# Hybrid decoder step: centred values in mLSTM and retention, the head norm taken on undivided numerators, and the four mLSTM denominators on four column tiles

## The reference, cut to what matters

```python
# mLSTM, per head; s = (q k^T) * W
num = einsum(s, v) + a_inter * einsum(q, C)
den = sum(s) + a_inter * einsum(q, n)
h   = num / maximum(abs(den), exp(-m_t))
C_new = a_old * C + einsum(w_end, k, v);  n_new = a_old * n + einsum(w_end, k)
# retention, per head
o = einsum(s, v) + cross
# both: norm over the 128 values of a head
xc = x - mean(x);  y = xc * rsqrt(mean(xc * xc) + eps) * gain
```

## Time and profile before

| what | value |
|---|---|
| median of three runs | 1513.43 us |
| lowest and highest run | 1510.20, 1519.79 us |
| span of the profiled execution | 1509.3 us |
| PE busy | 1479.3 us, 98% of the span |
| DVE, ACT, POOL busy | 770.5, 342.1, 56.2 us |
| DMA | 299.84 MB, mean 199 GB/s |

### The profile page before, as it was taken

How to read it: one execution, slowest core, us unless ns; L and a number is a source line. 1 busy time by engine, 2 the same in 40 slices (tenths; PEclk the granted TensorE clock), 3 DMA queues, 4 the chain that set the end, 5 groups by cost and what they waited for, 6 DMA issues and landing times.

```text
span 1509.3 us, 40728 instructions
## 1 busy us (share of the span) xinstructions
PE 1479.3 (98%) x17933; PEld 1265.3 (84%) x17933; DVE 770.5 (51%) x1700; ACT 342.1 (23%) x855; POOL 56.2 (4%) x68
## 2 busy tenths in 40 slices
PE   9999999999999999999999999999999899999997
PEld 6899976887899999998899977887888787888654
DVE  6446756746665655657366667636662211221123
ACT  2314224222212212233224224123130000000001
POOL 1000010110000000000000010200010000000000
PEclk9999999999999999999999999999999999999999
DMA  8324435203544354256524353114879998999993
GB/s 349 115 88 164 155 139 133 85 25 93 210 154 153 131 188 144 81 207 225 201 100 176 144 150 111 45 44 125 330 314 359 407 360 304 361 355 366 363 385 106
DMA packets 64335, 299.84 MB, mean 199 GB/s; under 512 B 21840, under 2 KB 23568, under 8 KB 37664
## 3 DMA queue, kind: packets, MB, share of 16 engines
q1 hardware_dynamic: 50392, 268.10, 48.5%
q0 software_dynamic: 2944, 18.09, 3.1%
q10 hardware_dynamic: 10823, 11.05, 2.7%
HBM read 277.93 MB, written 19.28 MB: 197 GB/s over the span
## 4 chain that ended last, share of the span: by engine, by line
PE 93%; DVE 3%; DMA 2%; issue 1%; ACT 1%; SPq 0%; DVEq 0%; ACTq 0%
PE ps L2112 15%; PE ps L1250 12%; PE ps L1913 12%; PE ps L1713 9%; PE ps L2035 7%; PE ps L1720 5%; PE ps L1199 4%; PE ps L1825 4%; PE ps L2009 3%; PE ps L1212 2%; PE ps L1787 2%; PE ps L1569 2%; DMA ring<-in_mix 2%; PE ps L1946 2%; PE ps L1265 1%
## 5 line engine op out<-in xcount | busy, mean ns | idle before, releaser
L1713 PE MATMUL ps<-xn,ring 128*128 128x288 f32 x576 | 155.7, 414 | 0.4 <-ACT gate L2478 0.4
L1713 PEld LDWEIGHTS ps<-xn,ring 128*128 128x128 f32 x576 | 105.9, 190 | 37.2 <-issue 10.3
L2112 PE MATMUL ps<-arena 128*128 128x144 f32 x1028 | 133.4, 286 | 1.2 <-DVE arena L3649 1.2
L2112 PEld LDWEIGHTS ps<-arena 128*128 128x128 f32 x1028 | 129.3, 190 | 1.4 <-issue 1.4
L1913 PE MATMUL ps<-y_ml,arena 128*64 128x96 f32 (+4 forms) x2688 | 111.7, 244 | 11.5 <-issue 11.4
L1913 PEld LDWEIGHTS ps<-y_ml,arena 128*64 128x64 f32 x2688 | 109.2, 137 | 15.2 <-issue 15.1
L2035 PE MATMUL ps<-arena,mixed 128*32 128x256 f32 x2024 | 111.3, 380 | 0.0
L2035 PEld LDWEIGHTS ps<-arena,mixed 128*32 128x32 f32 x2024 | 65.0, 110 | 42.3 <-issue 0.2
L3573 DVE TENSOR_TENSOR mixed<-ps,mixed 128x96 f32<-128x96 f32 (+4 forms) x66 | 16.8, 254 | 130.3 <-PE ps L1913 130.1
L1913 PEld LDWEIGHTS ps<-y_ml,ring 128*64 128x64 f32 x1536 | 62.1, 137 | 4.8 <-issue 4.8
L1913 PE MATMUL ps<-y_ml,ring 128*64 128x96 f32 (+4 forms) x1536 | 64.3, 245 | 0.6 <-issue 0.6
(11 more groups left out here) (588 smaller groups left out, 2554.4 us busy)
## 6 DMA issues: line engine op xcount, KB each, us to landing
arena<-in_egu SPq DMA_DIRECT2D x56, 1024.0 KB, 7.4
ring<-in_mix SPq DMA_DIRECT2D x46, 1024.0 KB, 5.5
arena<-in_edown SPq DMA_DIRECT2D x40, 1024.0 KB, 7.3
ring<-in_mix SPq DMA_DIRECT2D x48, 768.0 KB, 4.2
ring<-in_egu SPq DMA_DIRECT2D x32, 1024.0 KB, 7.5
ring<-in_gu SPq DMA_DIRECT2D x14, 1024.0 KB, 4.8
arena<-in_gu SPq DMA_DIRECT2D x8, 1024.0 KB, 5.1
arena<-in_C POOLq DMA_DIRECT2D x2, 2048.0 KB, 7.9
```

The costliest lines, as they stand in the source:

```text
L1713: last = mm(ps[:, bank, 0:T], ring[:, s, P * k:P * k + P], xn[:, k, :], start=(k == 0), stop=(k == KT - 1))
L2112: last = mm(ps[:, dense_bank(side, product), 0:HALF], left, right, start=(k == 0 and product in (1, 2, 5)), stop=(k == n - 1), skip_group_ ...
```

## The change

1. **Values are centred first.** The mean over a head's 128 values is taken off the values instead of off the outputs. DVE sums each token's values (`reduce_sum`, 128x1024 elements); POOL scales the eight sums by -1/128 and adds them to the values into a copy, `mvc` (in the space of `y_ret`) and `rvc` (in the space of `C0`). PE's numerators read the copies. The function `centre` on POOL runs twice a layer, and PE waits for it before the first numerator of each branch. For retention it also waits until the stores of the mLSTM states have landed.
2. **Samples.** Their outputs are centred by two DVE operations: in `sample_outputs` for mLSTM, and in place of ACT's copy for retention.
3. **No centring product.** `centred` is called for RWKV alone. ACT copies and squares each numerator straight out of PSUM.
4. **Denominators once.** PE broadcasts exp(-m) once for the four heads (to 32 rows a head) and makes the four heads' denominators in four column tiles of 32, after the last head. ACT takes one absolute value; DVE makes eps times the square of the denominator.
5. **The norm of the undivided numerator.** The root is taken of mean(num^2) + eps * den^2, so no head is divided by its denominator: three DVE operations a head go.
6. **State n rides with C.** A column of ones stands behind each head's values, so C and n come from one product of 129 columns.
7. **Order.** `COUPLES` becomes rq, rk, mo, mo, zrw 0, zrw 1, rg, rg, then zrw 2 to 6. The norm's steps move: the sums stand at `AT_MLNORM`, six parts lie before the spread; retention's sums stand before the stream's last two parts.

```diff
@@ PE, mlstm_head @@
-                mm(ps[:, 4, 0:TP], picked_head(h), rows[0:NH, 1, 0:TP], start=True, stop=True)
-                mm(ps[:, 5, 0:TP], picked_head(h), rows[0:NH, 2, 0:TP], start=True, stop=True).then_inc(ml_bc.sem, 1)
+                mm(ps[:, 4, 0:TP], picked_head(h), rows[0:NH, 1, 0:TP], start=True, stop=True).then_inc(ml_bc.sem, 1)
...
+                if h == 0:
+                    pe.wait_ge(*v_cent(l, 1))
...
-                for bank, part in ((7, "num"), (4, "den")):
-                    def left(i):
-                        return mvt[:, i, P * h:P * h + P] if part == "num" else C("ones", P)
-                    mm(ps[:, bank, 0:TP], left(0), ml_PW[:, 0:TP], start=True, stop=False, skip_group_check=True)
-                    last = mm(ps[:, bank, P:TP], left(1), ml_PW[:, TP:PW], start=False, stop=True, skip_group_check=True)
-                last.then_inc(ml_nd.sem, 1)
+                mm(ps[:, 7, 0:TP], mvc[:, 0, h, :], ml_PW[:, h, 0:TP], start=True, stop=False, skip_group_check=True)
+                mm(ps[:, 7, P:TP], mvc[:, 1, h, :], ml_PW[:, h, TP:PW], start=False, stop=True,
+                   skip_group_check=True).then_inc(ml_nd.sem, 1)
+
+            def mlstm_denominators(l):
+
+                mm(ps[:, 5, 0:TP], C("sel_s", P, NH), rows[0:NH, 2, 0:TP], start=True, stop=True)
+                for out, weights in ((slice(TP, 2 * TP), slice(0, TP)), (slice(TP + P, 2 * TP), slice(TP, PW))):
+                    for h in range(NH):
+                        last = mm(ps[sample(h), 5, out], C("ones", TS), ml_PW[:, h, weights], start=(out.start == TP),
+                                  stop=(out.start > TP), skip_group_check=True)
+                last.then_inc(ml_dn.sem, 1)
@@ PE, mlstm_state @@
-                for h in range(NH):
-                    for i in range(2):
-                        mm(ps[:, 5, h:h + 1], mkt[:, i, P * h:P * h + P], C("ones", 1), start=(i == 0), stop=(i == 1))
+                        mm(ps[:, 4 + h // 2 * 2, (P + 1) * (h % 2):(P + 1) * (h % 2) + P + 1], mkt[:, i, P * h:P * h + P],
+                           mvt[:, i, h, :], start=(i == 0), stop=(i == 1))
@@ PE, a layer @@
-                centred(3 * l, ml_o, C("cent128", P))
-                steps(l, AT_MLNORM, AT_MLNORM + 4)
+                pe.wait_ge(*ml_oe(l))
                 head_sums(3 * l, ml_sq, C("ones", TS))
-                steps(l, AT_MLNORM + 4, AT_MLNORM + 8)
-                head_spread(3 * l, ml_sq, C("lead", P))
-                steps(l, AT_MLNORM + 8, AT_ROTATE)
+                steps(l, AT_MLNORM, AT_MLNORM + 6)
+                head_spread(3 * l, ml_den, C("lead", P))
+                steps(l, AT_MLNORM + 6, AT_ROTATE)
...
-                centred(3 * l + 1, ret_o, C("cent128", P))
+                pe.wait_ge(*r_ote(l))
+                head_sums(3 * l + 1, ret_sq, C("ones", TS))
                 steps(l, AT_RNORM, NSTREAM)
                 fill(l, 6)
-                head_sums(3 * l + 1, ret_sq, C("ones", TS))
-                fill(l, 8)
-                head_spread(3 * l + 1, ret_sq, C("lead", P))
-                fill(l, 50)
+                head_spread(3 * l + 1, ret_sq[:, 0, :], C("lead", P))
+                fill(l, 58)
@@ ACT @@
-                A(ml_den, ps[:, 4, 0:TP], ACT.Abs).then_inc(ml_ad.sem, 1)
+                A(ml_o[:, h, 0:TP], ps[:, 7, 0:TP], ACT.Copy)
+                A(ml_sq[:, h, 0:TP], ps[:, 7, 0:TP], ACT.Square).then_inc(ml_h.sem, 1)
                 if h == 3:
+                    act.wait_ge(*ml_dn(l))
+                    A(ml_den[:, 0:TP], ps[:, 5, TP:2 * TP], ACT.Abs).then_inc(ml_ad.sem, 1)
...
+            def mlstm_norm(l):
+
+                projections(l, AT_MLNORM, AT_MLNORM + 2)
+                act.wait_ge(*ml_var(l))
+                A(ml_den, ml_den, ACT.Sqrt).then_inc(hn_q.sem, 1)
@@ DVE @@
-                dve.wait_ge(*ml_ad(l, h + 1))
-                link(TT(ml_den, ml_den, ps[:, 5, 0:TP], MAX))
-                link(dve.reciprocal(ml_den, ml_den))
-                TT(ml_o[:, h, 0:TP], ps[:, 7, 0:TP], ml_den, MUL).then_inc(ml_h.sem, 1)
+                if h == NH - 1:
+                    den = ml_den[:, 0:TP]
+                    dve.wait_ge(*ml_ad(l))
+                    link(STT(den, ps[:, 5, 0:TP], MOST, den, MIN, MAX))
+                    link(STT(den, den, GN_EPS, den, MUL, MUL))
...
+            def mlstm_norm(l):
+
+                dve.wait_ge(*hn_sum(3 * l))
+                STT(ml_den, ps[:, 4, 0:T], 1.0 / P, ml_den, MUL, ADD).then_inc(ml_var.sem, 1)
+                couple_add(l, 7, C12)
+                couple_sums(l, 9, 1, 2)
+                dve.wait_ge(hn_q.sem, 3 * l + 1)
+                dve.reciprocal(ml_den, ml_den).then_inc(hn_r.sem, 1)
+                couple_sums(l, 9, 2, 5)
@@ DVE, mlstm_gates after couple_sums(l, 2); mlstm_head h == 1 after kbm; retention after couple_add(l, 12, C11) @@
+                dve.reduce_sum(vsum.rearrange("p (i h) -> p i h", i=2), mvt[:, :, :, 0:P], axis=AX_X).then_inc(v_sum.sem, 1)
...
+                link(dve.reduce_sum(rosum, ps[:, 4, 0:P], axis=AX_X))
+                STT(ros, rosum.broadcast_to([P, P]), -1.0 / P, ps[:, 4, 0:P], MUL, ADD).then_inc(r_ose.sem, 1)
@@ POOL @@
+            def centre(l, n, values, centred, sums):
+
+                sums = sums.rearrange("p (i h) -> p i h", i=2)
+                pool.wait_ge(*v_sum(l, n))
+                pool.tensor_scalar(sums, sums, -1.0 / P, None, ALU.mult).then_inc(v_mean.sem, 1)
+                pool.wait_ge(*v_mean(l, n))
+                pool.tensor_tensor(centred, values, sums.unsqueeze(3).broadcast_to([P, 2, NH, P]), ALU.add)                    .then_inc(v_cent.sem, 1)
...
                 pool.dma_start(S0_ret, a["ret"][l]).then_inc(ld_ret.sem, 16)
+                pool.wait_ge(st_ml.sem, 64 * (l + 1))
+                by_head = [t.rearrange("p i (h e) -> p i h e", h=NH) for t in (rvt, rvc)]
+                centre(l, 4, *by_head, rvsum)
```

More of the change, by code:

```diff
@@ L78 @@
 NORM_EPS, GN_EPS, RW_GN_EPS = 1e-6, 1e-5, 64e-5
+MOST = 1.0e18
 RW_DECAY = 0.606531
@@ L380 @@
 GATE_BANK = (0, 2, 3, 1)
-COUPLES = [("rq", 0), ("rk", 0), ("mo", 0), ("mo", 1), ("rg", 0), ("rg", 1)] + [("zrw", i) for i in range(ZT // 2)]
-NCP = len(COUPLES)
 def projection_stream():
@@ L1277, in head_sums, with head_spread @@
                 last.then_inc(hn_tensor.sem, 1)
[L1279 removed]
+            def head_spread(q, roots, lead):
                 pe.wait_ge(hn_r.sem, q + 1)
                 for j in range(4):
[L1283 removed]
+                    last = mm(ps[:, 4 + j, 0:T], lead[rows_of(j)], roots[rows_of(j), :], start=True, stop=True)
                 last.then_inc(hn_tensor.sem, 1)
@@ L1393, in mlstm_state @@
                 pe.wait_ge(*ml_kb(l))
-                last = mm(ps[:, 5, 8:8 + SB * NH], kts, C("bsel", SB * NH), start=True, stop=True)
+                last = mm(ps[:, 4, 264:264 + SB * NH], kts, C("bsel", SB * NH), start=True, stop=True)
                 last.then_inc(ml_cp.sem, 1)
@@ L2275, in projection @@
                 else:
-                    if part < 2:
-                        dst = (mvt if kind == "mv" else rvt)[:, part, 256 * piece:256 * piece + 256]
-                    else:
-                        dst = (mvs if kind == "mv" else rvs)[:, 0:P]
-                    last = A(dst, ps[:, GROUP_BANK[n], 0:256 if part < 2 else P], ACT.Copy)
+                    if part == 2:
+                        last = A((mvs if kind == "mv" else rvs)[:, 0:P], ps[:, GROUP_BANK[n], 0:P], ACT.Copy)
+                    elif kind == "rv":
+                        last = A(rvt[:, part, 256 * piece:256 * piece + 256], ps[:, GROUP_BANK[n], 0:256], ACT.Copy)
+                    else:
+                        last = A(mvt[:, part, 2 * piece:2 * piece + 2, 0:P],
+                                 ps[:, GROUP_BANK[n], 0:256].rearrange("p (h e) -> p h e", h=2), ACT.Copy)
                 last.then_inc(evac.sem, 1)
@@ L2297, in projections, with retention_norm, rwkv_norm @@
                           scale=DK ** -0.5 if COUPLES[c][0] == "rk" else 1.0).then_inc(c_copy.sem, 1)
[L2299 to L2310 removed]
+            def mlstm_norm(l):
+                projections(l, AT_MLNORM, AT_MLNORM + 2)
+                act.wait_ge(*ml_var(l))
+                A(ml_den, ml_den, ACT.Sqrt).then_inc(hn_q.sem, 1)
+            def retention_norm(l):
+                act.wait_ge(*hn_sum(3 * l + 1))
+                A(ret_sq[:, 0, :], ps[:, 4, 0:T], ACT.Sqrt, scale=1.0 / P, bias=C("eps", 1, P, 1)).then_inc(hn_q.sem, 1)
+                projections(l, AT_RNORM, NSTREAM)
+                unit_gates(l, "norm")
+                unit_gates(l, "shift")
+            def rwkv_norm(l):
+                for j in range(4):
+                    act.wait_ge(*hn_x(l, j + 1))
+                    A(rw_sq[:, j, :], rw_o[:, j, :], ACT.Square).then_inc(hn_s.sem, 1)
+                act.wait_ge(*hn_sum(3 * l + 2))
+                A(rw_sq[:, 0, :], ps[:, 4, 0:T], ACT.Sqrt, scale=1.0 / CH, bias=C("eps", 1, P, 2)).then_inc(hn_q.sem, 1)
```

(25 more changed lines are left out.)

142 lines of the change are left out of this document (68 added, 74 removed).

## The result

The changed kernel takes 1502.99 us (median of 6 runs, 1500.31 to 1506.12), the kernel before 1513.61 (6 runs, 1509.41 to 1519.79). The ratio is 0.9925 with an interval of 0.9901 to 0.9949, so it is faster by 0.75%; the medians lie 10.6 us apart. The forecast was 1497.4, a gain of 16.0. The direction came true. The range, 1491.0 to 1503.0, holds the result by its last 0.01 us, which is luck: single runs of the changed kernel scatter by 5.8. The result lies outside the 1495 to 1499.5 that had the chance of 0.60, and a gain above 1%, which had 0.56, did not come either. A third of the forecast gain is missing, and most of what follows asks where it went.

What follows compares the result with a forecast made beforehand. PE's own list was taken to bound the kernel: 8.21 us a layer less, 16.4 in two, minus 0.4 for waits, gives 16.0 off 1513.43, so 1497.4 us. The range was 1491.0 to 1503.0.

Steps and rivals of the forecast that it cites:

- What bounds the kernel: Whole kernel: PE's own list sets the time, busy 1479.3 of 1509.3 us; loads follow PE.
- PE's own sum: Both layers: PE loses 9.90 us and gains 1.67 and 0.02, net 8.21 us a layer, 16.4 in two.
- rival (a): Denominator tiles do not overlap, or waits in heads 1, 2 or the norm open wider; about 1501 us, chance 0.22.
- Covers of DVE and ACT: Heads and norms: DVE's and ACT's supplies come about when PE needs them; the mLSTM norm's reciprocal is covered by 0.5 us.
- The three tight distances: DVE's supply to PE: head 1 late by 0.1 us, head 2 by 0 to 0.1, mLSTM norm covered by 0.5.
- New waits: Need against supply in the mLSTM and retention branches; all waits put at 0.2 us a layer (0 to 1.5).
- The signs it named: Trace signs: right if PE busy and span fall 16 us; wrong if named PE waits or 2.6 us tiles show.
- falls altogether: mLSTM heads to retention norm: fails if that stretch shrinks under 5 us a layer, or a later one grows.
- The clock: Half-clock dip at 757.00 to 760.00 in layer 1: costs at most 1.5 us, may go or come.
- (b): Experts' stage after 1118 us: loads paced by memory give the gain back; 1510 to 1514 us, chance 0.07.
- (c): POOL's second centring, for retention, is late and PE waits; slower from 19 us of delay a layer, chance 0.02.
- (d): More gain than forecast: added work overlaps, a dip goes, waits elsewhere shrink; 1491 to 1495 us, chance 0.09.

Runs made afterwards that it cites:

- d1: Changed kernel plus sixteen unread centring products on PE ahead of the mLSTM norm's sums, in layer 1 alone; 1514.31 us against 1507.27 for the changed kernel.
- a0: The changed kernel run again without any edit, as the base for experiments on its chip; 1507.27 us, ratio 0.9915 to the kernel before.
- b0: The kernel before the change, run once more for a second profile, which shows no dip of the clock; 1518.99 us.
- e1: Changed kernel with POOL centring retention's values ahead of its wait for y_ml and two loads, eleven us earlier; 1505.13 us, ratio 0.9900 to the kernel before.
- e2: Changed kernel with POOL's addition of the means split into eight 128x128 operations with one tensor input, same place; 1506.99 us, ratio 0.9914 to the kernel before.
- v2b: Changed kernel with the early centring and the two stream parts between heads 0 and 1 set apart, second run; 1505.98 us, ratio 0.9883 to the kernel before.
- p3: Changed kernel with POOL's addition for retention done three times in a row, PE waiting for the last; 1509.95 us, ratio 0.9935 to the kernel before.

## Why the prediction was right, and where it fell short

**What bounds the kernel: right.** d1 shows that time put into PE's list in layer 1 arrives at the end, and what the change takes out of it arrives too: the mixers of a0 are 12.2 us shorter than those of b0, and the medians lie 12.6 apart. For layer 0 no experiment added time; its share is in those two numbers.

**PE's own sum: right.** It said 8.21 us a layer. Up to the rotation the terms are L1364, the denominators, the one-column products and mLSTM's centring product less the additions, 1.72 + 2.60 + 1.68 + 1.95 - 1.69 = 6.26; measured 90.8 - 84.5 = 6.3. From the keys to the LoRA products it is retention's centring product, 1.95 forecast; the stretch goes from 60.52 (173.74 to 234.26) to 58.57, so 1.95. The new denominators with their broadcast, from which the sum drew its largest uncertainty:

```profile
115.61 0.39 PE L1384 MATMUL ps<-arena,y_ret 128*128 128x128 f32 x2
115.92 0.69 PE L1389 MATMUL ps<-arena,con 4*128 4x256 f32 x2
116.55 0.86 PE L1392 MATMUL ps<-arena,con 128*32 128x256 f32 x16
117.34 1.25 PE L1258 MATMUL ps<-xn,ring 128*128 128x144 f32 x8
118.42 1.14 PE L1258 MATMUL ps<-mixed,ring 128*128 128x144 f32 x8
```

The next part starts 1.42 us after the broadcast: 0.63 for the broadcast and 0.79 for the tiles, where 0.61 + 0.24 were taken by shape alone. The neighbours pay too. L1384 is followed after 0.31 us, where another one (106.51) is followed by a part after 0.22, and the part behind the tiles takes 1.08 to the next one instead of 0.98. With these 0.09 and 0.10 the price is 1.61, against 1.67 forecast and 3.42 without overlap. So the changes of shape do cost something, about what was charged, and it lies in the neighbours, not in the tiles' own rows. The first half of rival (a) falls.

**Covers of DVE and ACT: right.** The sum over tokens takes 1.21 us (forecast 1.23), and PE waits for nothing in the heads. Timeline of DVE in the changed kernel, with the norm's reciprocal:

```profile
94.58 1.21 DVE L2961 TENSOR_REDUCE arena<-arena 128x8 f32<-128x1024 f32 x1
147.69 1.95 DVE L2735 RECIPROCAL arena<-arena 128x288 f32<-128x288 f32 x1
```

and of PE, the spread that needs it:

```profile
150.41 0.77 PE L1289 MATMUL ps<-arena,con 32*128 32x288 f32 x8
```

The reciprocal ends at 149.64, 0.8 before the spread (forecast 0.5). The three tight distances all held, so the other half of rival (a) did not happen either. The time that it names, 1498.6 to 1503.5, holds the result, but by another cause and in another place.

**New waits: the failed step.** The sentence "The first numerator is at 181.62 ..., about 2 us earlier after the change relative to that load: 11 us hide it" asked only when PE needs the centred values. That was right, and PE never waits for POOL. It put nothing on the addition beyond POOL's own end, and left out what it does to DVE, which was costed as if alone. The term "0.2 a layer (0 to 1.5) on all waits" was 1.7 from this one cause, beyond its own upper bound. e1 shows the cause: the same addition, eleven us earlier, takes the whole 1.7 away. Of it, 1.23 are PE's idle time (12.50 less 11.27). The rest lies around the two gaps: the part ahead of each takes its full 1.14 us, where in a running stream the next one starts after 0.98, and the part behind each takes 1.08 to the next.

The rows to see it in were at hand. PE was without a wait in the stretch from rotation to keys, but DVE was busy for 10.63 of 10.80 us, and the earlier trace rows read busy time only for the heads, for 3 us of the clock and for the experts. A stretch in which a second engine is busy for 98% has no cover for anything that slows that engine.

The effect itself also stood in the trace of the kernel before, beside the very row from which the addition's price was taken, L3809 at 292.61 to 294.99 us. Timeline of DVE in the kernel before:

```profile
294.44 0.86 DVE L3236 TENSOR_TENSOR mixed<-mixed,gate 128x288 f32<-128x288 f32 x1
```

This product of two tensors in SBUF takes 0.46 us elsewhere, the median of its sixteen, and 0.86 here, and it ends 0.31 us behind POOL's. Three transposes with one input, which DVE ran beside the same POOL operation, took 0.40 to 0.70, as they do elsewhere.

The Trainium skill states the rule that speaks to this, in SBUF — State Buffer, section SBUF: two separate sides: VectorE and GpSimd share a pair of ports, and when a VectorE operation has two SBUF inputs and a GpSimd operation reads SBUF, whichever starts first keeps the pair for its whole instruction while the other waits. The trace agrees for the long addition, by the times given above: the block sum comes second and ends 0.54 us after POOL's end. It agrees less in e2, where L2794 starts 0.61 us into a POOL instruction that reads SBUF and loses 0.05 us; there the measurement decides. I had not weighed the rule.

**A second, smaller miss.** From the LoRA products of layer 0 to the first head of layer 1 the kernel before takes 503.1 and 502.9 us in two profiles, and all changed ones 503.6 to 503.9. A wait that the kernel before does not have stands in the closing products of layer 0, while another shrinks. PE in the kernel before and, behind it, in the changed one:

```profile
392.05 2.21 PE L1787 MATMUL ps<-arena 128*128 128x144 f32 x16 [0.75 <-DVE arena L3263]
```

```profile
386.62 2.21 PE L1797 MATMUL ps<-arena 128*128 128x144 f32 x16 [0.39 <-DVE arena L3321]
393.29 1.22 PE L1797 MATMUL ps<-xn,arena 128*128 128x144 f32 x8 [1.53 <-DVE arena L3335]
```

The addition L3335 stands in DVE's list behind sums of the dense weights. In the two kernels, in the same order, DVE reaches the loads of the dense weights at

```profile
395.38 1.29 DVE L3663 TENSOR_TENSOR arena<-arena 128x512 f32<-128x512 f32 x2 [1.31 <-DMA arena<-in_gu]
```

```profile
391.64 1.29 DVE L3721 TENSOR_TENSOR arena<-arena 128x512 f32<-128x512 f32 x2 [3.00 <-DMA arena<-in_gu]
```

Everything around is about 5 us earlier, the issue of this load too (380.78 against 385.85), but DVE can start on it only 3.7 us earlier. All the changed kernels have this wait, of 1.4 to 1.5 us, and neither profile of the kernel before has it. The prediction had said nothing of this stretch. Why the load takes longer to land wasn't settled; no experiment touched it, and it stays open.

**The sum, put together.** Here the stretches are taken between the starts of PE's instructions in b0 and a0, neither of which has a dip. Twice 6.23 and twice 1.95 gained, twice 1.71 lost between them, 0.80 lost in the closing: 12.46 + 3.90 - 3.42 - 0.80 = 12.14 us. The mixers say 12.15 by the same starts, and the medians beside a0 say 12.6. The first comparison says 10.6 with an interval of 7.7 to 15.0 (ratios 0.9949 and 0.9901 of 1513.6), which holds 12.1; the 1.5 us between them are not told from scatter. The forecast of 16.0 was therefore 3.9 too high by its own reckoning: 3.0 of it are the term of the waits (3.4 for 0.4), 0.8 the closing.

**The signs it named.** Those for right came in part: the broadcast takes 0.63 and the tiles 0.79, L1265's product runs in RWKV alone, and no wait of PE for POOL shows; but PE is busy for 13.3 us less, not 16. None of the four signs of a single rival came. There were two by which the prediction "falls altogether", and both came, the first if it is read as written. From the first head to the start of the retention norm the time goes from 125.36 us in b0 to 120.92 in a0, so it shrinks by 4.4, under the 5 named; with the norm's own centring product counted it is 6.4. And a later stretch grows, by the 0.8 of the closing. By its own signs, then, the prediction did worse than by its range.

**The clock: as bounded.** A dip in layer 1 went and one in layer 0 came between the two first profiles. Each is worth 1.3 us (92.10 less 90.80; 85.80 less 84.50), within the 1.5 allowed, so the dips explain none of the missing gain. e1's layer 0 lost 1.55, just over it.

**Rivals.** (b) is refuted by d1. (c) did not happen, and even with three additions PE did not wait for POOL: the wait that grows is another one. (d) did not happen. Nor does the early centring reach its 1491 to 1495: without dips its mixers would be 815.0 - 2 x 1.7 = 811.6, near the 811.9 of v2b, some 15.5 us below b0, so about the forecast's 16.0. With the step that failed taken out, the forecast is met but for the closing.

## What to carry to other kernels

Work moved to an idle GpSimd is not free for the VectorE work beside it: before giving it a place, read VectorE's timeline there, and put the move beside operations that read PSUM or have one tensor input (seen here for L3030 in p3 and for the transposes beside L3809), or where nobody waits for VectorE. When a stretch is judged by its busiest engine, read the second busiest too: here, at 98%, a stretch of 1.7 us in one of its instructions came out as 1.7 us of time. And where a forecast rests on removed instructions of the engine that bounds the kernel, a sum by rows is good to some tenths of a us; the error sits in the term called "waits".

## What the runs showed of the hardware

GpSimd's addition of two tensors of 128x1024 in SBUF, fp32, takes 1.90 to 2.31 us (L3830), and a VectorE operation with two SBUF tensors of 128x512 that comes second ends about 0.55 us after it: 2.15 to 2.39 us in place of 0.69 in the places shown (starts 67.19 and 161.88 in the changed kernel, 150.60 in e1). VectorE operations with one tensor in PSUM are not held (L3030, 1.54 us for four with and without), nor are transposes with one input. In the other direction, GpSimd's operation of 8 columns takes 0.69 in place of 0.25 beside a block sum, and its one-input operation of 128x128 up to 1.54 in place of 0.60, at a loss to VectorE of at most 0.09. Eight products on four column tiles, with a left factor of 128x32 and 256 and then 128 columns, take 0.79 us together; the full-array part behind them takes 0.10 more than usual, and the product ahead of their 4-row broadcast 0.09.
